# A two-block transformer kernel on one core: constant products in seven waits of TensorE, and one weight split and one rotation moved in the last layer

## What is computed

```python
def first_block(...):            # one layer
    sh1, sc1, g1, sh2, sc2, g2 = adaln_params(c, w_mod, b_mod)      # silu(c) @ w_mod, six parts
    h = rmsnorm(x, n1) * (1 + sc1) + sh1
    q, k, v, gb, gcv, u, ga, gv = split_proj(h @ w_in)
    y_attn = windowed_attention(q, k, v, kc, vc, sink) @ w_attn_out # kc, vc from the context
    y_conv = conv_branch(gb, gcv, u, conv_w, w_conv_out)
    x = x + g1 * merge_branches(y_attn, y_conv, ga, gv, w_mix_out)
    h2 = rmsnorm(x, n2) * (1 + sc2) + sh2
    x = x + g2 * peer(h2, pw_q, p_keys, p_u, p_v)    # 128 chosen experts a token, gathered rows
...
def second_block(...):           # two layers, l = 0 and l = 1
    h = rmsnorm_2(x, attn_norm[l])                   # l = 1: keys and values from a norm of their own
    if l < N_A:                                      # l = 0
        o = moba_attention(q, k, v)
    else:                                            # l = 1, four key heads, window of 128
        o = swa_sink_attention(q, shared_k, shared_v, sinks_b[i])
    x = x + o @ w_o
    x = x + conv_ffn(rmsnorm_2(x, ffn_norm[l]), w_up[l], conv_w[l], conv_b[l], w_down[l])
```

## Time and profile before

| | |
|---|---|
| median of 3 runs | 1572.59 us |
| lowest and highest | 1567.46 and 1580.56 us |
| profiled execution, its own time | 1571.96 us |
| its span, first to last instruction | 1569.9 us |
| TensorE busy | 1408.3 us, 90% |
| VectorE, ScalarE, GpSimd busy | 1064.7, 773.5, 299.0 us |
| mean granted TensorE clock | 0.968 of full |

### The profile page before, as it was taken

One profiled execution on the slowest core, in us unless ns is written; L12 is line 12 of the kernel. 1 busy time (PEld: TensorE's weight loads), 2 busy tenths in 40 slices (PEclk: granted clock), 3 DMA queues, 4 the chain that ended last, 5 costly groups with the idle time before them and its releaser, 6 DMA issues.

```text
span 1569.9 us, 21949 instructions
## 1 busy us (share of the span) xinstructions
PE 1408.3 (90%) x7848; PEld 1045.6 (67%) x7848; DVE 1064.7 (68%) x2253; ACT 773.5 (49%) x1644; POOL 299.0 (19%) x297
## 2 busy tenths in 40 slices
PE   6999998899998788788778789989999998999998
PEld 4989996444442223223222388989999987989997
DVE  2778675766666667666665577547777776477776
ACT  3555533444444444444444364745555566355555
POOL 0011001444554444444444200000000010000000
PEclk9999998999999999999999999999999998899999
DMA  9666755999999999999999944235555431255553
GB/s 396 226 215 215 251 191 214 402 426 422 426 427 427 427 427 427 427 427 427 427 426 427 425 148 159 82 107 177 176 183 186 162 134 54 95 178 183 187 183 129
DMA packets 62585, 432.91 MB, mean 276 GB/s; under 512 B 7072, under 2 KB 7584, under 8 KB 12192
## 3 DMA queue, kind: packets, MB, share of 16 engines
q0 software_dynamic: 41616, 285.76, 43.9%
q1 hardware_dynamic: 20160, 145.37, 26.4%
q10 hardware_dynamic: 720, 0.62, 0.1%
HBM read 430.67 MB, written 1.05 MB: 275 GB/s over the span
## 4 chain that ended last, share of the span: by engine, by line
PE 58%; DMA 22%; DVE 9%; ACT 8%; issue 2%; POOL 0%; SPq 0%; ACTq 0%; DVEq 0%; POOLq 0%
PE banks L675 25%; PE banks L1083 13%; DMA arena<-in_peer_uv,experts 11%; DMA tok_b<-in_peer_uv,experts 5%; PE banks L712 4%; PE banks L1251 3%; PE banks L1219 3%; DVE wlow L1770 3%; DMA tok_a<-in_peer_uv,experts 2%; PE banks L886 2%; PE banks L927 2%; ACT diag L1538 2%; DMA arena<-in_w_mod 1%; ACT whigh L1295 1%; PE banks L846 1%
## 5 line engine op out<-in xcount | busy, mean ns | idle before, releaser
L1083 PE MATMUL banks<-arena,diag 128*128 128x512 f32 x780 | 383.3, 626 | 78.5 <-ACT diag L1538 77.9
L1770 DVE TENSOR_TENSOR wlow<-wring,whigh 128x1024 fp32r<-128x1024 f32 x234 | 275.8, 1220 | 113.5 <-ACT whigh L1295 113.3
L2198 DVE CUSTOM_DVE_ANT_0 arena<-arena,scores 128x1024 f32<-128x1024 f32 x200 | 245.1, 1225 | 158.6 <-DMA arena<-in_peer_uv,experts 156.8
L1083 PEld LDWEIGHTS banks<-arena,diag 128*128 128x128 f32 x780 | 141.4, 194 | 307.9 <-ACT diag L1538 180.7
L1295 ACT ACTIVATE whigh<-wring 128x1024 fp32r<-128x1024 f32 x234 | 234.3, 1048 | 98.3 <-DMA wring<-in_w_down 32.2
L1719 POOL DMA_INDIRECT arena<-in_peer_uv,experts x200 | 217.4, 1087 | 306.8 <-PE banks L1083 256.8
L675 PE MATMUL banks<-f_high,whigh 128*128 128x256 f32 x720 | 205.2, 285 | 8.5 <-DVE wlow L1770 5.4
L675 PE MATMUL banks<-f_low,whigh 128*128 128x256 f32 x720 | 203.7, 283 | 0.0
L675 PE MATMUL banks<-f_high,wlow 128*128 128x256 f32 x720 | 203.7, 283 | 0.0
L1530 ACT ACTIVATE dots<-dots 128x1 f32<-128x1 f32 x256 | 51.8, 202 | 302.0 <-DVE dots L2198 301.8
L675 PE MATMUL banks<-a_high,whigh 128*128 128x256 f32 x512 | 153.9, 301 | 10.2 <-DVE a_low L1814 7.0
(11 more groups left out here) (284 smaller groups left out, 2417.6 us busy)
## 6 DMA issues: line engine op xcount, KB each, us to landing
wring<-in_w_up SPq DMA_DIRECT2D x44, 1024.0 KB, 4.9
wring<-in_w_down SPq DMA_DIRECT2D x22, 1024.0 KB, 4.9
wring<-in_w_in SPq DMA_DIRECT2D x17, 1024.0 KB, 5.5
wring<-in_w_qkv_a SPq DMA_DIRECT2D x12, 1024.0 KB, 5.0
arena<-in_w_mod SPq DMA_DIRECT2D x8, 1024.0 KB, 16.6
arena<-in_w_mod_t POOLq DMA_DIRECT2D x16, 512.0 KB, 4.8
hT<-in_w_mod_t POOLq DMA_DIRECT2D x16, 512.0 KB, 5.4
wring<-in_peer_w_q SPq DMA_DIRECT2D x5, 1024.0 KB, 5.0
```

What stands on the lines that cost most here:

```text
L1083: mm = nc.tensor.matmul(banks[:, 2 + 2 * b + half, :], diag[:, n % DIAGS, :], ring[ROW_PLACE[n]][:, D + half * 512:D + (half + 1) * 512], ...
L1770: V.tensor_tensor(low, w, high.bitcast(F32), ALU.subtract).then_inc(w_split, 1)
L2198: V.tensor_tensor_reduce(out=ring[ROW_PLACE[n]][:, 0:D], in0=ring[ROW_PLACE[n]][:, 0:D], in1=h2tok[:, b, :], scale=1.0, scalar=0.0, op0=AL ...
```

## The change

The change does three things. It puts 37 more constant products of 128 by 256 into TensorE's stream: seven in the opening stage (one more in the old place, one between each of chunks 5 to 8 and its turn, two behind the fifth turn), two ahead of and seven behind the norm sum in front of the first query product, eight in front of the slots of l = 0, six in front of the first `wo_rows` of l = 0, four in front of `ffn_down_banks`, and three in slot 2 of l = 1. In `wo_rows` of both layers the wait for `o_ready` is moved behind the other two, ahead of the constant products' place. In l = 1 the last `rotate` goes from the head of slot 12 to a place between `turn_probs` and `score` of that slot. And in l = 1 ScalarE and VectorE leave out the splitting of a chunk at the end of slot 11 and do it at the end of slot 13; it is the third chunk of the output matrix `w_o_b_2`.

```diff
--- before.py
+++ after.py
@@ -724,6 +724,11 @@
 
             norms = 0
 
+            def constant_products(count, bank):
+
+                for _ in range(count):
+                    nc.tensor.matmul(banks[:, bank, 0:T], averaging, const[:, 0:T], start=True, stop=True)
+
             def norm_sum(src=hT):
 
                 nonlocal norms
@@ -795,11 +800,6 @@
                 if g == 3:
                     mm.then_inc(proj_made, 1)
 
-            def constant_products(count, bank):
-
-                for _ in range(count):
-                    nc.tensor.matmul(banks[:, bank, 0:T], averaging, const[:, 0:T], start=True, stop=True)
-
             pe.wait_ge(ident_in, 16)
             norm_sum()
             pe.wait_ge(cond_ready, 1)
@@ -808,10 +808,13 @@
                 if p > 0:
                     mod_turn(p - 1)
             mod_turn(KT // 2 - 1)
-            constant_products(4, 4)
+            constant_products(5, 4)
             for p in range(KT // 2, KT):
                 mod_chunk(p)
+                constant_products(1, 4)
                 mod_turn(p)
+                if p == KT // 2:
+                    constant_products(2, 4)
                 if p > KT // 2:
                     first_projection(p - KT // 2 - 1)
             first_projection(3)
@@ -898,7 +901,7 @@
                                              ident)
                 mm.then_inc(quad_turned, 1)
 
-            def attention_slot(plan, slot):
+            def attention_slot(plan, slot, ahead_of_scores=None):
 
                 at = plan["at"]
                 if slot - BACK in at and at[slot - BACK]["last"]:
@@ -907,6 +910,8 @@
                     weigh(plan, at[slot - WEIGH])
                 if slot - TURN in at:
                     turn_probs(at[slot - TURN])
+                if ahead_of_scores is not None:
+                    ahead_of_scores()
                 if slot in at:
                     score(plan, at[slot])
 
@@ -1002,8 +1007,10 @@
                 mm = tile_pair(g % 4, c, high_low[0], (merge_ready, 0) if i == 0 else None)
                 mm.then_inc(mix_made, 1)
                 g += 1
+            constant_products(2, 5)
             norm_sum(x_squares)
             pe.wait_ge(keys_in, 16)
+            constant_products(7, 5)
 
 
             def key_scores(h):
@@ -1148,15 +1155,19 @@
                     m += 1
 
                 plan, chunks2 = plans[1 + l], len(proj2[l])
+                if l == 0:
+                    constant_products(8, 2)
                 for slot in range(plan["slots"]):
                     n, j = divmod(slot, 2)
+                    if l == 1 and slot == 2:
+                        constant_products(3, 6)
                     if n < chunks2:
                         project(n, j)
                     if l == 0 and slot == 2:
                         norm_sum_added(cT)
                     if l == 1 and slot == 2:
                         norm_sum_added()
-                    if slot == 2 * chunks2:
+                    if l == 0 and slot == 2 * chunks2:
                         rotate()
                     if l == 1 and slot == 5:
 
@@ -1167,13 +1178,15 @@
                                              start=True, stop=True).then_inc(dup2_made, 1)
                     if l == 1 and slot == plan["first"]:
                         pe.wait_ge(dup2_read, 1)
-                    attention_slot(plan, slot)
+                    attention_slot(plan, slot, rotate if l == 1 and slot == 2 * chunks2 else None)
                     early = slot - (plan["first"] + 11)
                     if 0 <= early < 3:
 
-                        pe.wait_ge(o_ready, 4 + 4 * l)
                         pe.wait_ge(roped2, r)
                         pe.wait_ge(proj2_read, m)
+                        if early == 0:
+                            constant_products((6, 0)[l], 0)
+                        pe.wait_ge(o_ready, 4 + 4 * l)
                         pe.wait_ge(score_read, plan["groups"][-1]["n"] + 1)
                         wo_rows(l, min(early, 1), ((0, 1), (0,), (1,))[early])
                 pe.wait_ge(o_ready, 6 + 4 * l)
@@ -1224,6 +1237,7 @@
 
                 def ffn_down_banks(i):
 
+                    constant_products(4, 6)
                     pe.wait_ge(ff_ready, i + (f0 + 1))
                     halves = [down_pair(i, kk, True) for kk in range(2)]
                     for t in range(KT):
@@ -1622,7 +1636,7 @@
                         act.wait_ge(dup2_made, 4)
                         copy(flat(kdup2[:, :, :]), banks[:, 6:8, :].rearrange("p b n -> p (b n)")).then_inc(dup2_read, 1)
                     attention_slot(plan, slot)
-                    if j == 1 and n < chunks2:
+                    if j == 1 and n < chunks2 + l and (l, n) != (1, chunks2 - 1):
                         round_next()
                 for _ in range(2):
                     round_next()
```

## The result

| | before | after |
|---|---|---|
| median | 1572.34 us, 7 runs | 1559.87 us, 7 runs |
| lowest and highest | 1566.18 and 1580.56 | 1557.03 and 1562.75 |
| ratio after / before, 95% interval | | 0.9918 [0.9889, 0.9948] |
| profiled execution, span | 1571.96, 1569.9 | 1558.91, 1556.8 |
| mean granted TensorE clock | 0.968 | 0.983 |

The change makes the kernel 0.8% faster; 1561 was forecast.

What follows compares the result with a forecast made beforehand. TensorE was taken to bound the kernel (58% of the chain, DMA 22%), running at half clock behind holes. Terms summed to 11.0 us: 1571.96 - 11.0 = 1561.0 us, forecast 1561, range 1553 to 1572.

Steps and rivals of the forecast that it cites:

- The opening, 2.4: Opening stage: two rounds at full clock start the eighth chunk at 33.5 instead of 35.93 us, gain 2.4 us.
- My upper end of 2.9: Opening stage: 2.9 us gained if the product ahead costs nothing.
- Norm and first query, 3.5: Norm sum and first query at full clock: 0.4 us at the sum, 3.05 at the query's 32 records, together 3.5.
- the gathers hide it: Rival, chance 0.08: DMA bound from before the first gather, so the norm's 3.5 us goes; 1564.5 us.
- First projection, 0.5: First projection, l = 0: clock could gain 2.4 us, but the norm's sum waits for VectorE's squares; gain 0.5.
- Output product, 2.2: First output product, l = 0: 48 matmuls, 8.02 us before, at full rate; gain 2.2 us.
- Down product, 1.5: Down product: 20 records take 2.4 us at full rate, not 3.6; with the parts before and after, gain 1.5.
- slot 2, 1.4: Second chunk, l = 1: 18 records take 2.16 us at full rate, not 3.5; gain 1.4 us.
- holes by chance: Rival, chance 0.20: clock falls behind the 0.87, 1.36 and 2.11 us holes are luck, nothing gained there; 1566 us.
- The moves, -0.5: l = 1: g5's maxima end some 3.7 us sooner, given back before g7's maxima; 0.5 us lost.
- The moves pay: Rival, chance 0.12: normalising and the third chunk's split overlap better, g7 starts up to 4 us sooner; 1556.5 us.
- The sum: All places: 2.4 + 3.5 + 0.5 + 2.2 + 1.5 + 1.4 - 0.5 = 11.0 us gained.

Runs made afterwards that it cites:

- no long holes: Changed kernel without the products about norm and first query, before the first projection and before the first output product of l = 0: 1562.42 us, ratio 0.9953.
- the narrow run: Changed kernel with each constant product of 256 columns given as four products of 64 columns: 1580.32 us, ratio 1.0065 to the kernel before.

## Why the prediction was right, and where it was not

**The opening, 2.4.** Right in the profiled pair: the sixth chunk 0.65 late where 0.45 was reckoned, the stage 27.22 to 24.84, the eighth chunk 2.2 sooner. Its size by the median is larger, 6.7 to 7.5. The profile of before showed the shorter of two losses, as did two others without the products (2.3 to 2.7 us), and one showed 5.6. My upper end of 2.9 was too low: it was drawn from one execution.

**Norm and first query, 3.5.** 3.2 in the profiles: 2.98 at the 32 records (3.05 reckoned), 0.2 and not 0.4 at the sum. Removing the nine products alone cost 3.0. The shift passed through the gathers whole: their first row moved by 7.1 us and their last by 7.1, so "the gathers hide it" falls.

**First projection, 0.5.** 0.4 by the chain. The norm's sum waits for squares as was said:

```profile
917.94 1.13 PE L751 MATMUL banks<-hT,const 128*128 128x256 f32 x4 [1.06 <-DVE hT L1821]
```

Eight products buy next to nothing here, because VectorE's split and the squares behind it stand on the chain up to this sum.

**Output product, 2.2.** 2.0 in the profiled pair. Without its products the profile of "no long holes" lost only 1.0, so the median worth is less.

**Down product, 1.5, and slot 2, 1.4.** 1.49 and 1.36 in the profiled pair. For slot 2 all three profiles without its products have the loss (13.89, 13.88, 13.76 against 12.53); for the down product two of three have it. There the rival "holes by chance" holds in part, and the 1.5 is worth less in the median.

**The moves, -0.5.** -0.33 to the second turn of heads, -0.35 in all. g5's maxima come 3.66 sooner (3.7 was said), and g7's 0.34 later (0.5). The mechanism was the one named: ScalarE rounds behind g6's exponentials, and VectorE's split of 2.36 and a normalising stand ahead of g7's maxima. "The moves pay" falls by both kernels that try it.

**The sum.** 11.0 forecast, 12.5 by the medians, 13.05 by the profiled executions, of which the edited places have 10.2. The rest is from places not edited, which the sum left out because it took one profile's half clock elsewhere as fixed: two stretches of clock ahead of the gathers, and loads. The first stretch is luck: the changed kernel's repeat had half clock there again (granted clock 0.60 over 94 to 98 us). By the medians of the kernels with parts removed, the opening and the other short holes carry 7.7 where 5.3 was reckoned, the long ones 2.5 to 3.3 where 6.2 was. That the total came out within 2 us is partly luck, because these misses have opposite signs.

**Whether the place varies.** The prediction weighed the Trainium skill, "TensorE: Matmul & The Clock Gate", section "What's actually happening", by which the place of the clock's change varies from run to run. The traces agree with that: the down product's clock, the output product's behind a hole of 1.9 us, the length of the opening's half clock (6.3 us or 17) and column B changed from one execution to another with the code just ahead alike. The rival made from it erred in taking "varies" for "costs nothing in most runs": without its products the opening was at half in all four profiles that had none.

Open is why the opening is worth as much as 7 us in the median when three of four profiles lose 2.3 to 2.7 there and one 5.6, and whether the rotation alone, with the split at its old place, would keep its 1.43; that kernel was not run.

## What to carry to other kernels

In this kernel short holes of TensorE cost time beyond their own length: behind the 0.87 us ahead of the sixth chunk another 2.4 were lost, behind 2.11 us ahead of the down product another 1.5. Look in the stretches for half clock behind a hole, and put work that nobody reads into it. Price the place from several executions, since one profile shows one of its two or three outcomes. Size the filler to end just ahead of the wait; with half of it one run kept full clock in all six places, and another lost two of them. A move that frees an engine early is worth nothing if its own work lands in front of the next thing waited for on that engine.

## What was not expected of the hardware

In one profile holes of 0.50 to 0.59 us between chunks were enough in the opening: without the added products the clock fell to 1.2 GHz at about 27.5 us, and it stayed there for 17 us in spite of 12.89 us of busy time in 13.90. These are the rows of the two holes ahead of it, and of the one in which it fell:

```profile
24.98 0.61 PE L781 MATMUL banks<-const,mod_row 128*128 128x2 f32 x4 [0.50 <-ACT mod_row L1306]
26.17 1.07 PE L770 MATMUL banks<-arena,csil 128*32 128x256 f32 x16 [0.59 <-DMA arena<-in_w_mod]
27.75 1.01 PE L781 MATMUL banks<-const,mod_row 128*128 128x2 f32 x4 [0.50 <-ACT mod_row L1306]
```

The Trainium skill ("TensorE: Matmul & The Clock Gate", section "HAM oscillation — how this bites in real kernels") has the fall come from one long wait between bursts of matmuls; in this case it also came behind several short ones, and in the narrow run in the middle of products without a hole, so busy time alone doesn't foretell the clock. The loss then lasts: from the second turn of heads on, 13.6 us of unbroken work ran at half clock, and the same work at full clock, once the holes ahead of it were filled.
